# Three plain gate and value pairs instead of two at the head of the 768-token FFNs, before Strassen's scheme begins

## The reference

```python
def conv_ffn(h, P):                       # h: tokens x 1024, w_gate and w_val: 1024 x 2816, w_down: 2816 x 1024
    gt = dwconv(h @ P["w_gate"], P["ffn_conv_w"], P["ffn_conv_b"])      # 3 taps along the tokens
    return (jax.nn.silu(gt) * (h @ P["w_val"])) @ P["w_down"]
...
x_ctx = x_ctx + cmod[5] * conv_ffn(h2c, P)        # 256 tokens
x_lat = x_lat + g2 * conv_ffn(h2, P)              # 512 tokens
```

## Time and profile before

| | us |
|---|---|
| median of 3 runs | 3483.11 (3477.84 to 3484.3) |
| profiled execution | 3485.82 |
| its span, first to last instruction | 3484.0 |
| mean granted TensorE clock, as a share of full speed | 0.986 |

### The profile page before, as it was taken

One profiled execution on the slowest core, in us unless ns is written; L12 is line 12 of the kernel. 1 busy time (PEld: TensorE's weight loads), 2 busy tenths in 40 slices (PEclk: granted clock), 3 DMA queues, 4 the chain that ended last, 5 costly groups with the idle time before them and its releaser, 6 DMA issues.

```text
span 3484.0 us, 47705 instructions
## 1 busy us (share of the span) xinstructions
PE 3285.4 (94%) x18173; PEld 2726.9 (78%) x18173; DVE 2328.7 (67%) x3810; ACT 1485.6 (43%) x2432; POOL 433.1 (12%) x388
## 2 busy tenths in 40 slices
PE   7998989999999889999998888999998999999998
PEld 5775779999977677888886577999997866678886
DVE  4767378988878647778335748888886555565345
ACT  3336354434444544233234545444444444444233
POOL 2005200000000453000003521000001033200000
PEclk9999999999999999999999999999999999999999
DMA  6440123444222125556221212334531311123332
GB/s 212 133 127 13 38 73 109 124 134 154 84 78 62 31 72 128 190 165 195 67 60 25 44 31 80 103 114 135 154 101 49 70 28 31 37 73 104 90 102 74
DMA packets 452930, 321.90 MB, mean 92 GB/s; under 512 B 55128, under 2 KB 418046, under 8 KB 452704
## 3 DMA queue, kind: packets, MB, share of 16 engines
q1 hardware_dynamic: 442784, 304.14, 29.4%
q0 software_dynamic: 9920, 14.71, 1.8%
HBM read 313.20 MB, written 3.57 MB: 91 GB/s over the span
## 4 chain that ended last, share of the span: by engine, by line
PE 72%; DVE 14%; ACT 5%; issue 5%; DMA 3%; POOL 1%; DVEq 0%; SPq 0%; ACTq 0%; POOLq 0%
PE PS L1392 69%; PE PS L1860 3%; DVE CPROD L3547 2%; DMA MS<-in_mod_turned 2%; DVE TMP L4017 1%; DVE RINGL L3600 1%; ACT BIG L2596 1%; DVE HL L3243 1%; DVE ATT L3367 1%; DVE TMP L3645 1%; DVE TMP L3102 1%; ACT SPH L2205 0%; DVE SPL L3034 0%; DVE X L3482 0%; DVE TMP L3235 0%
## 5 line engine op out<-in xcount | busy, mean ns | idle before, releaser
L1392 PE MATMUL PS<-HH,SPH 128*128 128x512 f32 (+1 forms) x2024 | 724.3, 367 | 34.5 <-ACT HH L2405 10.7
L1392 PE MATMUL PS<-HL,SPH 128*128 128x512 f32 (+1 forms) x2024 | 701.2, 363 | 5.0 <-DVE HL L3243 2.3
L3034 DVE TENSOR_TENSOR SPL<-RAW,SPH 128x1024 fp32r<-128x1024 f32 (+3 forms) x256 | 306.5, 1197 | 316.6 <-ACT SPH L2205 316.4
L1392 PEld LDWEIGHTS PS<-HH,SPH 128*128 128x128 f32 x2024 | 385.3, 190 | 119.6 <-issue 38.9
L1392 PE MATMUL PS<-HH,SPL 128*128 128x512 f32 (+1 forms) x2024 | 465.3, 365 | 0.0
L1392 PEld LDWEIGHTS PS<-HL,SPH 128*128 128x128 f32 x2024 | 380.6, 190 | 67.8 <-DVE HL L3243 9.6
L1392 PEld LDWEIGHTS PS<-HH,SPL 128*128 128x128 f32 x2024 | 354.5, 190 | 66.5 <-issue 7.6
L2205 ACT ACTIVATE SPH<-RAW 128x1024 fp32r<-128x1024 f32 (+3 forms) x256 | 264.0, 1031 | 299.1 <-PE PS L1392 227.1
L3547 DVE CUSTOM_DVE_ANT_0 CPROD<-MS,CB 128x1024 f32<-128x1024 f32 x224 | 274.0, 1223 | 40.8 <-DMA MS<-in_mod_turned 23.1
L3367 DVE TENSOR_REDUCE ATT<-PS 128x1 f32<-128x768 f32 x160 | 146.1, 952 | 119.8 <-PE PS L1392 119.6
L1392 PE MATMUL PS<-HH,RINGH 128*128 128x384 f32 x640 | 215.9, 337 | 6.2 <-DVE HQL L3572 5.3
(11 more groups left out here) (497 smaller groups left out, 6522.9 us busy)
## 6 DMA issues: line engine op xcount, KB each, us to landing
MS<-in_mod_turned SPq DMA_DIRECT2D x144, 512.0 KB, 4.5
RAW<-in_l_w_up SPq DMA_DIRECT2D x48, 512.0 KB, 3.8
RAW<-in_w_in SPq DMA_DIRECT2D x40, 512.0 KB, 4.7
MS<-in_w_mod SPq DMA_DIRECT2D x32, 512.0 KB, 4.8
RAW<-in_l_w_in SPq DMA_DIRECT2D x26, 512.0 KB, 3.8
RAW<-in_w_gate SPq DMA_DIRECT2D x24, 512.0 KB, 4.2
RAW<-in_w_val SPq DMA_DIRECT2D x24, 512.0 KB, 4.0
RAW<-in_w_down SPq DMA_DIRECT2D x16, 704.0 KB, 4.6
```

What stands on the lines that cost most here:

```text
L1392: return pe.matmul(o, a, b, start=start, stop=stop, skip_group_check=onto_read)
L3034: dve.tensor_tensor(wlo(t)[:, 0:kc, :], raw_place(t)[:, 0:kc, :], whi(t)[:, 0:kc, :].bitcast(F32), ALU.subtract).then_inc(S.lo_ready, 1)
```

## The change

`HEAD_F` becomes 3. Chunk 2 of each 768-token FFN is then computed by two plain tiles, as chunks 0 and 1 are, and 19 pairs go through Strassen's scheme. The second edit keeps a job of the second block's 512-token FFN (the scaling of the residual, which stands in ACT's head work at j = 4 to 11) out of the 768-token head, which now also has tiles 4 and 5; there the scaling stays where it was, in `fast_ffn`.

```diff
-HEAD_F, TAIL_F = 2, 16
+HEAD_F, TAIL_F = 3, 16
...
-                        if blk == 1 and half == 0 and 4 <= j < 4 + DC:
+                        if blk == 1 and half == 0 and not L["fast"] and 4 <= j < 4 + DC:
                             act.wait_ge(S.gains_ready, (1, 3)[li - 2])
                             residual_scale(j - 4, T)
```

## The result

| | before | after |
|---|---|---|
| median of 13 runs each, us | 3482.67 (3476.36 to 3485.81) | 3487.99 (3480.96 to 3494.17) |
| ratio, 95% interval | | 1.002 (1.0012 to 1.0028) |
| profiled execution, us | 3485.82 | 3485.9 |
| its span, us | 3484.0 | 3484.1 |
| mean granted clock | 0.986 | 0.988 |

The account below looks back on a forecast made before the run. TensorE, busy 94% of the span, was taken to bound the kernel. Seams -3.5, clock falls +4.85 and late slab +3.2 gave +4.5 us on the median of 3483.11: 3487.6 us, 8-in-10 range 3477 to 3496.

Parts of the forecast that it names:

- wait in front of tile 4: Head: tile 4's split queues on ScalarE behind tile 2's SiLU; waits of 1.95 and 3.66 us in the two FFNs.
- unit 2: First Strassen pair: due at T + 12.52 us (T: end of tile 4), ready at T + 11.03, so no wait.
- wait at unit 3: First Strassen pair: due at T + 14.60 us, ready at T + 16.96 (T: end of tile 4); waits 2.36 us in both FFNs.
- wait in the second pair, first FFN: Second Strassen pair: the old wait of 1.48 us stays, as the ScalarE job behind it is bound to a step.
- loss in the second pair, second FFN, with the clock: Second Strassen pair: three units of 2.08 us take 12.20 us, so 5.96 us are lost, as before.
- falls of the clock after the four new waits: Tile 4 and unit 3, both FFNs: 2.3 us after the 3.66 us wait, 0.85 after each other; +4.85 us, bounds 0 to 11.8.
- seams: End of head to first down unit: 51.63 and 57.82 us without new clock falls, together -3.5; 52 to 54, 59 to 61 expected.
- wait for the late slab: Before each FFN's last unit: second tail slab loads late, 1.6 us each, +3.2 us for two FFNs (2.7 to 4.7).
- sum: Whole kernel: -3.5 at the seams, +4.85 for the clock, +3.2 for the tail slab; +4.5 us.
- A: Seams: third pair hides the whole preparation; -6.2 and -7.7, tail +3.2, so -10.7 us and 3472.4 us; chance 0.10.
- B: Tile 4 and unit 3, both FFNs: a long clock fall after each wait, 11.8 us; total +11.5, 3494.6 us; chance 0.15.
- C: Seams: preparation only moves along, old losses of 9.8 and 15.8 us stay; +13.1 us, 3496.2 us; chance 0.07.

Follow-up runs that it names:

- kernel with the sums at tile 2: Changed kernel with VectorE's four sums of h made after its taps for tile 2, not after tile 1; 3476.28 us, ratio 0.9989 to the kernel before.
- slab-released one: Changed kernel with one sum at tile 1, three at tile 2, the first two sums' splits behind tile 5's split; 3470.97 us, ratio 0.9976.
- the first four experiments: Changed kernel with sums at tile 2 (0.9989), second tail slab in an earlier-free buffer (1.0016), preparation spread over the head (0.9991), the last two together (0.9969).

## Why the prediction was right

The time came out 0.4 us from the forecast of 3487.6. That is partly chance: the falls of the clock were taken too small by 1.9 us, and the loss in the second pair too large by 1.3 us, as the terms show (us, where one number stands for both FFNs together):

| step of the prediction | forecast | measured |
|---|---|---|
| wait in front of tile 4 | 1.95 and 3.66 | 1.97 and 3.60, from the end of tile 3 |
| unit 2 | no wait | no wait |
| wait at unit 3 | 2.36 in both | 2.29 in both |
| wait in the second pair, first FFN | 1.48 | 1.48 |
| loss in the second pair, second FFN, with the clock | 5.96 | 10.86 - 6.24 = 4.62 |
| falls of the clock after the four new waits | 4.85 | 6.71 |
| seams | 52 to 54, 59 to 61 | 55.34, 59.85 |
| wait for the late slab | +3.2 | +2.9 |
| sum | +4.5 | +1.84 + 0.38 + 2.9 = +5.1 by the profile, +5.3 by the medians |

*The pair swap and the waits.* Every wait was found at the place, behind the engine and at nearly the size that the old timelines gave. The kernel with the sums at tile 2 shows the cause of the first; the slab-released one shows that unit 3 hangs on what VectorE and ScalarE do around the last gate tile.

*The clock.* This is the term that was mis-sized. Half of 1.71 us was taken for each wait but the longest, because rows of both kinds were there. One row that it shows was left out of that count: behind the wait of 3.60 us unit 3 started at 0.62 us, and by unit 4's row in the same timeline it took 517.31 - 513.60 = 3.71 us in place of 2.08:

```profile
517.31 0.34 PE L1392 MATMUL PS<-T1H,RINGH 128*128 128x384 f32 x1
```

The prediction also passed over a wait of 1.74 us at unit 3 of the second FFN of the kernel before, where the granted clock was low too (0.55 from 2175.8 to 2179.7 us). In the execution shown all four were followed by a fall, so the first seam missed its range by 1.3 us. In the second FFN the old fall behind the second pair's wait was 4.62 - 3.01 = 1.61 us and not 2.95, and that made up for most of it.

*The late slab.* The times from issue to landing of the tail slabs' transfers in the kernel after (shortest, median, longest) are near the 3.2 us that were taken:

```profile
DMA to landing us min/median/max: 3.1/3.3/3.4
```

The waits were 1.42 and 1.5 us, against 1.6. The prediction's estimate of 2.9 us from the Trainium skill (DMA: Bandwidth & Descriptors, section on the anatomy of one DMA, measured for the GpSimd path) would have given 1.05; the row was nearer.

*The rivals.* A, in which the third pair hides the whole preparation, does not hold for the change as made, for the two reasons given against it; it is the kernel that one gets when both are mended: 0.9976 and, with the slab, 0.9965, where A's 3472.4 us, which hold the late slab, would be 0.9969. Of B one half held in the execution shown: all four waits were followed by a fall, but of 1.64 to 1.71 us each and never 2.95, and their 6.71 us stay under the 7.3 from which it was to decide. The Trainium skill (TensorE: Matmul & The Clock Gate, section on oscillation) describes a kernel in which every group of matmuls behind a wait begins at the lower clock; the waits there are longer than most of these, and the prediction carried it over to short ones. With that reading these four waits agree only in part: a fall follows each, but unit 3 begins at 0.41 us and falls afterwards. Others do not agree. Behind the wait of 1.48 us at 546.34 the clock stays at 1.00, as it does behind unit 3's 2.29 us in the kernel with the sums at tile 2. Even the second pair's 3.01 us, followed by a fall in the kernels before and after, was not in the slab-released one, where its last three units took 6.34 us (2.08 us each without a wait) at a clock of 1.00:

```profile
2200.47:2206.81 6.34, 6.34 (x36) 6.34 (x37) 3.61 (x6) 5.49 (x9) 0.00 (x0) 1.00 0.01 3
```

C, that the preparation only moves along, is excluded by unit 2, which doesn't wait.

Why the change costs 0.2%, then: it gives VectorE a tile pair of room at 2.16 us in each FFN, while the four sums stay at j = 1 and the other preparation hangs on the last gate tile. The waits in front of units 2 and 3 are exchanged for others in front of tile 4, at unit 3 and in front of the last unit, with a fall of the clock behind each at the seam. What remains open is which waits are followed by a fall: 2.29 us was in one kernel and not in another, and the same holds for 3.01 us.

## What to carry to other kernels

Room on the busiest engine is worth something only if the work that was late can start in it: look in each list of instructions for what the new gap would let go first, and move that in the same edit. A move that brings work forward also pushes something back, here a split that releases a load; ask of each instruction that is moved past another what the other one releases, the transfers above all. And a time that hangs on a buffer's parity (here the second tail slab, late because the number of loads became odd) is worth a look whenever a count changes.

## What the runs showed of the hardware

Short waits in a dense stream of matmuls can cost more than their length: in the kernel after, the fall of the clock behind 1.81 us of idle cost 1.71 us, behind 2.29 us 1.66, behind 3.43 us 1.70. At these places the price hardly depended on the length of the wait, but behind one and the same wait of 3.01 us it was 2.95 us in the kernel before, 1.61 in the kernel after and nothing in the slab-released one. So neither whether there is a fall nor its price is settled by the length of the wait alone. The clock differs between executions elsewhere in the kernel too (0.80 and 0.93 in the same 25 us of two of them), and this goes with runs of one kernel that lie up to 19 us apart: of the 31 runs of the kernel before beside the first four experiments, the three at a mean granted clock of 0.985 took 3487 us on average and the eight at 0.989 or 0.990 took 3476.
